# Rows read once without a copy, no normalisation behind the last layer, filler pieces spread over all steps

## The reference

```
h = rms_norm(x, norm_g[l])
q, k, v, gate_a, f, u, vb, gate_b, g_a, g_b = split(h @ w_in[l])      # q, k normed per head; f -> log forget
attn  = forgetting attention of 8 heads (causal; score + c[q] - c[k], softmax, @ v)
s_sgu = causal 128-chunk mixing of vb
m = sigmoid(g_a) * ((attn * silu(gate_a)) @ w_pa) + sigmoid(g_b) * ((u * s_sgu * silu(gate_b)) @ w_pb)
x = x + m @ w_o
```

## Time and profile before

| | |
|---|---|
| median of 3 runs | 2194.61 us |
| the profiled execution | 2196.81 us, span 2194.8 us |
| PE busy | 1959.1 us (89%), 11260 matmuls |
| DVE, ACT, POOL busy | 999.8, 698.3, 492.7 us |
| mean granted TensorE clock | 0.954 |

### The profile page before, as it was taken

The page is one execution under the profiler, slowest core; times in us unless marked ns, Lnnn a source line. Parts: engine busy times, 40 slices in busy tenths (PEclk is TensorE's granted clock), DMA queues, the critical chain, the costliest instruction groups (busy, mean ns, idle before and its releaser), DMA issues. The chain is left out here.

```text
span 2194.8 us, 31311 instructions
## 1 busy us (share of the span) xinstructions
PE 1959.1 (89%) x11260; PEld 1793.9 (82%) x11260; DVE 999.8 (46%) x2358; ACT 698.3 (32%) x1523; POOL 492.7 (22%) x508
## 2 busy tenths in 40 slices
PE   2789999999696999898978999999987699989898
PEld 2689999999575889897858998989975588989886
DVE  3345545455455334445434454554544533444543
ACT  3233343434332322203223343343343232221131
POOL 1432323232011112202015132333201021121110
PEclk9999999999897999999989999999998899999999
DMA  5332132311113322423223223132112153224241
GB/s 170 74 99 56 52 94 60 92 49 48 58 45 101 108 76 69 150 106 125 101 77 82 74 55 93 48 87 57 42 41 77 48 145 87 69 84 156 91 154 43
DMA packets 216877, 183.39 MB, mean 84 GB/s; under 512 B 50164, under 2 KB 186884, under 8 KB 216724
## 3 DMA queue, kind: packets, MB, share of 16 engines
q1 hardware_dynamic: 216724, 181.39, 28.5%
HBM read 132.17 MB, written 49.17 MB: 83 GB/s over the span
## 5 line engine op out<-in xcount | busy, mean ns | idle before, releaser
L71 PE MATMUL bank<-keep_hhi,at_fhi 128*128 128x384 f32 (+1 forms) x768 | 264.1, 344 | 17.3 <-ACT at_th L754 17.3
L73 PE MATMUL bank<-keep_hhi,at_flo 128*128 128x384 f32 (+1 forms) x768 | 256.2, 334 | 0.0
L72 PE MATMUL bank<-keep_hlo,at_fhi 128*128 128x384 f32 (+1 forms) x768 | 256.2, 334 | 0.0
L71 PE MATMUL bank<-at_whi,keep_hhi 128*128 128x384 f32 (+3 forms) x576 | 200.7, 349 | 18.0 <-POOL at_wlo L838 16.7
L71 PE MATMUL bank<-keep_hhi,br_whi 128*128 128x384 f32 (+1 forms) x576 | 196.9, 342 | 20.8 <-POOL br_wlo L1109 20.8
L72 PE MATMUL bank<-at_wlo,keep_hhi 128*128 128x384 f32 (+3 forms) x576 | 198.0, 344 | 0.0
L73 PE MATMUL bank<-at_whi,keep_hlo 128*128 128x384 f32 (+3 forms) x576 | 197.5, 343 | 0.0
L72 PE MATMUL bank<-keep_hlo,br_whi 128*128 128x384 f32 (+1 forms) x576 | 190.5, 331 | 0.0
L73 PE MATMUL bank<-keep_hhi,br_wlo 128*128 128x384 f32 (+1 forms) x576 | 190.3, 330 | 0.0
L800 ACT ACTIVATE at_prob<-at_prob,at_nmx 128x128 f32<-128x128 f32 (+7 forms) x128 | 99.5, 777 | 273.2 <-DVE at_nmx L982 273.1
L71 PEld LDWEIGHTS bank<-keep_hhi,at_fhi 128*128 128x128 f32 x768 | 148.5, 193 | 20.6 <-ACT at_th L754 18.7
(11 more groups left out here) (240 smaller groups left out, 4473.0 us busy)
## 6 DMA issues: line engine op xcount, KB each, us to landing
mg_gate<-gates SPq DMA_DIRECT2D x32, 544.0 KB, 6.6
at_stage<-in_w_in SPq DMA_DIRECT2D x128, 128.0 KB, 2.5
at_stage<-in_w_in SPq DMA_DIRECT2D x64, 192.0 KB, 2.6
gates<-at_th SPq DMA_DIRECT2D x64, 192.0 KB, 2.3
br_stage<-in_w_in SPq DMA_DIRECT2D x48, 256.0 KB, 3.3
at_decay<-ncum SPq DMA_DIRECT2D x16, 512.0 KB, 3.9
br_k<-in_cache_k SPq DMA_DIRECT2D x32, 256.0 KB, 3.0
br_v<-in_cache_v SPq DMA_DIRECT2D x32, 256.0 KB, 3.1
```

What stands on the lines that cost most here:

```text
L71: nc.tensor.matmul(out, sh, mh, start=start and i == 0, stop=False)
L72: nc.tensor.matmul(out, sh, ml, start=False, stop=False)
L73: last = nc.tensor.matmul(out, sl, mh, start=False, stop=stop and i == n - 1)
```

## The change

It has three parts. In the rows phase, x is no longer copied to y; there are four buffers, and the gains are loaded behind the second tile. The output phase of the first layer reads the residual rows from x. In the last layer the output phase leaves out everything from the square on, and the load of gains. In the plan, the number of half pieces placed since the loop began (`fill.at - first`) takes the place of the counter's own count.

```diff
+def x_rows(g, t):
+    return row(g.xp2, t) if t < PT_ else g.xs2[:, :]
 def rows_phase(nc, g, sem):
-    xt = R("x", [P, 2, D])
+    NX = 4
+    xt = R("x", [P, NX, D])
...
-            sp.dma_start(gain[:, :], g.gains[0:1, :].to_broadcast([P, D])).then_inc(consts, 16)
-            def load(t):
-                if t >= 2:
-                    sp.wait_ge(y_out[t % 2], 16 * (t // 2))
-                    sp.wait_ge(hn_r, t - 1)
-                    sp.wait_ge(ss_r, t - 1)
-                src = row(g.xp2, t) if t < PT_ else g.xs2[:, :]
-                sp.dma_start(xt[0:ROWS[t], t % 2, :], src).then_inc(x_in[t % 2], 16)
-            load(0)
-            load(1)
             for t in range(NT):
-                sp.wait_ge(x_in[t % 2], 16 * (t // 2 + 1))
-                sp.dma_start(y_rows(t), xt[0:ROWS[t], t % 2, :]).then_inc(y_out[t % 2], 16)
-                if t + 2 < NT:
-                    load(t + 2)
-            sp.wait_ge(y_out[0], 16 * ((NT + 1) // 2))
-            sp.wait_ge(y_out[1], 16 * (NT // 2))
+                if t >= NX:
+                    sp.wait_ge(hn_r, t - NX + 1)
+                    sp.wait_ge(ss_r, t - NX + 1)
+                sp.dma_start(xt[0:ROWS[t], t % NX, :], x_rows(g, t)).then_inc(x_in[t % NX], 16)
+                if t == 1:
+                    sp.dma_start(gain[:, :], g.gains[0:1, :].to_broadcast([P, D])).then_inc(consts, 16)
...
 def output_phase(nc, l, g, sem):
+    normed = l + 1 < DEPTH
...
             def load(t):
                 if t >= NX:
                     sp.wait_ge(y_out[t % NX], 16 * (t // NX))
-                    sp.wait_ge(hn_r, t - NX + 1)
-                sp.dma_start(xt[0:ROWS[t], t % NX, :], y_rows(t)).then_inc(x_in[t % NX], 16)
+                    if normed:
+                        sp.wait_ge(hn_r, t - NX + 1)
+                sp.dma_start(xt[0:ROWS[t], t % NX, :], y_rows(t) if l else x_rows(g, t)).then_inc(x_in[t % NX], 16)
...
-                if u == 7:
+                if u == 7 and normed:
                     sp.dma_start(gain[:, :], g.gains[bass.ds(l + 1, 1), :].to_broadcast([P, D])).then_inc(consts, 16)
...
+            if not normed:
+                return
             for t in range(NT):
                 act.wait_ge(y_ready, t + 1)
...
                 last.then_inc(y_ready, 1)
+                if not normed:
+                    continue
...
-                if t:
+                if t and normed:
                     transposes(t - 1)
-            transposes(NT - 1)
+            if normed:
+                transposes(NT - 1)
...
 def attention_plan():
-    left = sum(2 * (s[0] == "Z") for v in after.values() for s in v) + len(fill.pieces) - fill.at
-    total, spent = left, 0
+    first = fill.at
+    total = sum(2 * (s[0] == "Z") for v in after.values() for s in v) + len(fill.pieces) - first
+    spent = 0
...
-        while spent < total * (n + 1) / (len(steps) + 1) and fill.at < len(fill.pieces):
+        while spent + fill.at - first < total * (n + 1) / (len(steps) + 1) and fill.at < len(fill.pieces):
             fill.half()
-            spent += 1
```

More of the change, by code:

```diff
@@ L91, in rows_phase @@
     hps = [[g.bank[4], g.bank[5]], [g.bank[6], g.bank[7]]]
-    x_in = [S("x0"), S("x1")]
-    y_out = [S("y0"), S("y1")]
+    x_in = [S(f"x{i}") for i in range(NX)]
     consts = S("consts")
@@ L96, in rows_phase @@
                                                     S("hlo"), S("own"))
-    def y_rows(t):
-        return row(g.yp2, t) if t < PT_ else g.ys2[:, :]
     with nc.Block() as block:
@@ L133, in _ @@
             for t in range(NT):
-                act.wait_ge(x_in[t % 2], 16 * (t // 2 + 1))
+                act.wait_ge(x_in[t % NX], 16 * (t // NX + 1))
                 if t:
@@ L138, in _ @@
                         act.wait_ge(ms_r, t - 1)
-                nc.scalar.activation(sqj[0:ROWS[t], :], xt[0:ROWS[t], t % 2, :], ACT.Square,
+                nc.scalar.activation(sqj[0:ROWS[t], :], xt[0:ROWS[t], t % NX, :], ACT.Square,
                                      accum_out=ss[0:ROWS[t], t % 2:t % 2 + 1]).then_inc(ss_r, 1)
@@ L179, in _ @@
                     dve.wait_ge(tr_r, t - 1)
-                nc.vector.scalar_tensor_tensor(hn[0:n, t % 2, :], xt[0:n, t % 2, :], rs[0:n, t % 2:t % 2 + 1],
+                nc.vector.scalar_tensor_tensor(hn[0:n, t % 2, :], xt[0:n, t % NX, :], rs[0:n, t % 2:t % 2 + 1],
                                                gain[0:n, :], ALU.mult, ALU.mult).then_inc(hn_r, 1)
@@ L332, in _ @@
                                                ALU.mult, ALU.subtract).then_inc(m_lo, 1)
-            dve.wait_ge(consts, 16)
+            if normed:
+                dve.wait_ge(consts, 16)
             for t in range(NT):
@@ L353, in _ @@
                                                gain[0:n, :], ALU.mult, ALU.mult).then_inc(hn_r, 1)
-            evac(NT - 1)
+            if normed:
+                evac(NT - 1)
         @block.tensor
```

## The result

The changed kernel takes 2161.57 us (median of 4 runs, 2160.95 to 2164.5). Beside it on the same chip the kernel before took 2195.99 us (median of 4, 2191.47 to 2199.61). The ratio is 0.9845, with a 95% interval of 0.9832 to 0.9859: 34 us less. The forecast was 2164.9 us, in a range of 2152 to 2182. The profiled execution took 2161.27 us (span 2159.6), against 2196.81 us (span 2194.8) before, and the mean granted clock went from 0.954 to 0.965.

The account below looks back on a forecast made before the run. TensorE was taken as the kernel's clock. Rows -0.3, output -10.6 and two attention layers -18.8 sum to -29.7 us: 2167.1 for the profiled execution, 2164.9 for the median, range 2152 to 2182.

Parts of the forecast that it names:

- The rival that only the output tail pays: Early attention steps expose as much as late ones recover: 2181 to 2187 us, 2184 worked out; chance 0.16.
- Rival B: Attention: both weight stretches speed up and piece-less steps stay covered, -15 us per layer, 2148 to 2157; chance 0.13.
- Rival C: Attention: freed early steps leave each piece's whole time idle, +31 us per layer, 2246 in all; chance 0.04.
- Rival D: Attention plan ends as before, the change doesn't spread: attention term 0, time as if only the output tail pays; chance 0.01.
- Rows phase: Tile pitch stays 5.99 us, removed stores give 0; only the first `ms` moves: -0.3 us, range -1 to +3.
- the in-order end of my range: Rows phase: if transfers are served in order, `gain` as third lands at about 10.2 and `ms` comes up to 1.0 us sooner.
- Output phase: Last layer: seven groups of transposes go, 6.5 us, and the last store becomes the end; gain 10.6 us. First layer's: 0.
- Attention, tail: Steps 81 to 97: pieces fill 9.5 us of TensorE holes and avoid 2.2 of slow clock, -11.7 per layer.
- Attention, early steps: Steps that lose their piece outrun DVE and ACT and expose waits, priced by today's piece-less pairs: +3.5 us per layer.
- the rest: Early attention steps other than 60/61, 34/35, 54/55 and 14/15 that lose pieces: +0.3 us together.
- Attention, the two stretches: Weight-split steps 20 to 25 and 44 to 49: one piece leaves each, +2.1 us in the first, -3.3 in the second.
- The sign that was to show it: A TensorE wait of 3 to 6 us near step 25, and none over 3 us in steps 44 to 49.

Follow-up runs that it names:

- counter-only kernel: Kernel before with only the new counter in the attention plan: 2175.32 us, ratio 0.9912 to the kernel before.
- the last experiment: Changed kernel with the share of pieces raised to the power 1.3, so fewer early and more towards the tail: 2178.91 us, ratio 0.993.
- pieces-held kernel: Kernel before with the last four half pieces of its spread held back and put behind steps 84 (three) and 85 (one): 2185.07 us, ratio 0.9962.
- the kernel with six pieces: Changed kernel with one extra half piece behind each of steps 17, 20, 37, 44, 56 and 61, taken from the end of the spread: 2141.26 us.
- the kernel with both edits: Changed kernel with gate weight units of steps 20-24 and 44-48 postponed and six extra half pieces per layer placed at waits: 2128.42 us, ratio 0.9705.

## Why the prediction was right

**The whole.** -29.7 us forecast, -34 measured (some 2 of them scatter of the unchanged phases), time inside the forecast's own 2160 to 2173. The rival that only the output tail pays (2184) fell with the counter-only kernel: 19.3 us of the gain are attention. Rival B, in which both weight stretches speed up (2153.7 worked out), failed on the first stretch, which grew, as the argument against it had said. Rival C, in which the early steps lose more than the late ones win, 31 us a layer, names a cost that exists (the last experiment), but at 7.0 us for ten pieces and not at the whole 2.1 of each. Rival D fell with the tail, which is full. That the attention term came out so close for layer 1 is in part luck, as its terms below show: errors of 2.2 us in one and of 2.4 in the others cancel.

**Rows phase: a step failed, without weight.** Forecast -0.3, measured +0.2. The step that failed was "`gain` as the third is there at about 10.2": it landed at 11.49, while x0 was there for ScalarE at 8.18 instead of 10.00. Its issue to landing rose from 4.6 to 6.2 us. The sign of the term can't be told: with `gain` third the first `ms` lies between 11.11 and 11.51 in six traces, with the old order between 11.25 and 11.28 in four. With `gain` second it landed at 9.68. So the place in the queue matters, as the in-order end of my range had it, but as the third it landed 1.3 us later than that end said; whether x2 and x3 behind it took this share was not tried. The pitch of 5.99 us did not move when two buffers became four and nine stores went, as said.

**Output phase: right in both terms, one of them by a cancelling error.** -6.5 forecast and -6.3 measured up to the last add, -4.1 and -4.2 behind it. The store did become the end. But the forecast let the end follow 3.2 us behind its issue, and it took 4.0; it also counted the old end from 2193.93 where the span ends at 2194.8. The two misses, 0.8 and 0.9 us, cancel. The first output phase kept its 79.61 us, as said.

**Attention, tail: right.** Forecast -11.7 a layer: 9.5 of holes (all gone) and 2.2 of clock. The pieces-held kernel measures 2.4 for that clock, and 5.49 us busy at 0.50 gives 2.7.

**Attention, early steps: size near, places half wrong.** Forecast +3.5, measured +2.2: step 61 with 1.10 (forecast 1.2), 17 with 0.48 more (0.5), and 41 and 65 with 0.32 and 0.31 (within "the rest"). Steps 34 to 37 got no more than they had (forecast +1.0), nor 54 to 57 (+0.5). Whether two steps hold a piece gave the right price for a single empty pair and overrated a second one in front of it.

**Attention, the two stretches: right in sign, the first at half its size.** By TensorE's waits, the first costs 2.9 us (1.49 in steps 21 and 22, which I had not named, and 1.45 more at step 25), and its clock 1.4 more than before (3.1 against 1.7), so +4.3 against +2.1. The step that failed is "In the first that only makes the hole longer": the term held the moved piece alone and neither the G units that come into step 23 nor the clock. The second gives 1.0 of waits (3.01 down to 2.02, of which 1.53 are new at steps 45 and 46) and the 2.9 of clock, so -3.9 against -3.3; its length is 24.66 us where I had 24.5. That in the first stretch the G units "now land where they hurt in the second today" stood only against rival B, outside the sum; holding them back showed it. The sign that was to show it, one wait of 3 to 6 us near step 25, came as two waits of 2.52 and 2.96 us.

**The sum of a layer.** Layer 1: -12.2+2.2+4.3-3.9 is -9.6, measured -9.7 from the V of step 2 to the last V, forecast -9.4. Layer 2 gained 13.0, which is 3.6 more than forecast. Its busy time fell by the same 4.5 us as in layer 1, its idle time by 8.5 us and not 5.3. Most of the difference is the wait in step 25: 5.48 us in layer 1 and 3.89 (0.93 and 2.96) in layer 2, where the two G splits wait 2.45 and 0.60 us for their DMA, not 2.71 and 1.95. Before, the same stretch had waits of 4.03 in layer 1 and 5.11 in layer 2 (its last two weight splits waited 2.19 and 2.21 us for their DMA, in layer 1 2.25 and 0.88). So in layer 2 the wait fell by 1.2 us where that of layer 1 grew by 1.45. Why the DMA of these units is late by different amounts in the two layers was not tried.

## What to carry to other kernels

Filler pays where the main engine waits, not where a counter puts it: an even spread recovered 19 us, six pieces a layer moved into the measured waits 19.5 us more (0.0089 of 2194.24), with the shift of weight splits that came along. Read the waits of the new trace and move one piece to each; then look for new ones, since pieces taken from a neighbour open its own. Keep work that waits on a DMA and is wanted late out of an in-order engine's list ahead of work that the main engine waits for: such splits cost 4.3 us of stretch and 2.9 us of clock in the first stretch of layer 1, and a new plan that frees one place of them may put them in another.

## What the runs showed of the hardware

The clock behind a wait: after 4.87 us of waiting it was granted 0.50 over 576.00 to 581.67, and after 2.52 and 2.96 us with 2.6 us between them it was 0.50 over 283.78 to 289.31. This cost 2.4 and 2.9 us beside the waits (11.01 us for what takes 8.60, 11.21 for what takes 8.32). After 2.68 us in the kernel with six pieces it was 0.67 over 281.82 to 287.00:

```profile
281.82:287.00 5.18, 5.17 (x24) 5.04 (x25) 1.22 (x6) 1.74 (x6) 1.30 (x2) 0.67 0.37 118
```

Much shorter waits can be followed by it too, and need not be. In the kernel with more pieces towards the tail it was 0.66, 0.64 and 0.67 over the 5 us behind waits of 2.07, 2.45 and 1.69 us. In the kernel with six pieces a wait of 2.08 us in layer 2 was followed by 1.00:

```profile
1323.97:1330.00 6.03, 6.03 (x38) 5.94 (x39) 2.00 (x10) 2.74 (x8) 2.54 (x2) 1.00 0.35 99
```

With the pieces held for the tail, waits of 0.79 and 0.81 us in steps 80 and 81 of layer 2 were followed by 0.50 over 6.8 us, and the same waits in layer 1, with one of 2.07 us in step 82 behind them, by 1.00. Between the V of step 2 and the last V of the kernel with both edits, where no wait is above 0.33 us, it was 1.00 throughout.

The Trainium skill (TensorE: Matmul & The Clock Gate, Part 1) has idleness return the array to half rate; these rows agree, and show that the length of a wait alone doesn't say whether the clock falls or how much follows. What I had not expected is how much of a filler's worth this is: nearly half of layer 1's gain (4.5 of 9.7 us) was not idle time.
